# Head norms of the mixer stage: root by exponential of a logarithm, sums by one full matmul

## What is computed

```python
def _norm_f32(x):
    return x * lax.rsqrt(jnp.mean(x * x, axis=-1, keepdims=True) + EPS)
...
h = h + _hybrid_mixer(_rmsnorm(h, mix_norm_w[l]), positions, w_in[l], gdn_conv_w[l], ...,
                      hgrn_norm_w[l], w_out[l])
h = h + _memory_cross_attn(_rmsnorm(h, xattn_norm_w[l]), mem_n, ...)
```

## Time and profile before

| | us |
|---|---|
| median of 3 runs | 2463.57 |
| lowest, highest | 2463.51, 2466.93 |
| the profiled execution, whole | 2461.06 |
| its span of instructions | 2459.3 |
| TensorE busy (matmuls) | 2359.7 (96%) |
| VectorE busy | 1683.5 (68%) |
| ScalarE busy | 681.1 (28%) |
| GpSimd busy | 139.2 (6%) |

### The profile page before, as it was taken

One profiled execution on the slowest core, in us unless ns is written; L12 is line 12 of the kernel. 1 busy time (PEld: TensorE's weight loads), 2 busy tenths in 40 slices (PEclk: granted clock), 3 DMA queues, 4 the chain that ended last, 5 costly groups with the idle time before them and its releaser, 6 DMA issues. The chain is left out here.

```text
span 2459.3 us, 35706 instructions
## 1 busy us (share of the span) xinstructions
PE 2359.7 (96%) x14784; PEld 1911.8 (78%) x14784; DVE 1683.5 (68%) x2643; ACT 681.1 (28%) x1239; POOL 139.2 (6%) x128
## 2 busy tenths in 40 slices
PE   8998859999999999999999899999999999999997
PEld 6886658977888888887755688888888888888886
DVE  6674466756888865558888686666666886666653
ACT  2321363022211101424677503222102113222200
POOL 0000002001000011000211010000010001000001
PEclk9999679999999999999999999999999999999999
DMA  4220003412232364212200171222562541322341
GB/s 180 77 77 3 21 2 129 146 52 78 95 102 94 128 207 145 88 67 82 73 10 2 55 271 65 98 94 95 184 223 89 205 180 61 103 94 95 132 137 65
DMA packets 70193, 252.44 MB, mean 103 GB/s; under 512 B 7792, under 2 KB 8080, under 8 KB 69520
## 3 DMA queue, kind: packets, MB, share of 16 engines
q1 hardware_dynamic: 69744, 249.63, 29.9%
q10 hardware_dynamic: 288, 0.54, 0.1%
HBM read 248.04 MB, written 2.10 MB: 102 GB/s over the span
## 5 line engine op out<-in xcount | busy, mean ns | idle before, releaser
L385 PE MATMUL psum<-rounded_n,rounded_high 128*128 128x512 f32 x1856 | 739.0, 398 | 4.4 <-DVE rounded_n_low L539 1.8
L386 PE MATMUL psum<-rounded_n_low,rounded_high 128*128 128x512 f32 x1856 | 726.3, 391 | 0.0
L387 PE MATMUL psum<-rounded_n,rounded_ring 128*128 128x512 f32 x1856 | 726.2, 391 | 0.0
L339 DVE TENSOR_TENSOR rounded_ring<-ring,rounded_high 128x1024 fp32r<-128x1024 f32 (+1 forms) x360 | 445.7, 1238 | 43.5 <-ACT rounded_high L322 31.5
L385 PEld LDWEIGHTS psum<-rounded_n,rounded_high 128*128 128x128 f32 x1856 | 350.6, 189 | 85.2 <-issue 7.2
L386 PEld LDWEIGHTS psum<-rounded_n_low,rounded_high 128*128 128x128 f32 x1856 | 350.7, 189 | 76.5 <-issue 5.5
L387 PEld LDWEIGHTS psum<-rounded_n,rounded_ring 128*128 128x128 f32 x1856 | 350.4, 189 | 73.7
L337 DVE CAST rounded_high<-ring 128x1024 fp32r<-128x1024 f32 (+1 forms) x347 | 248.8, 717 | 187.3 <-PE psum L387 180.1
L385 PE MATMUL psum<-rounded_arena,rounded_high 128*128 128x512 f32 x720 | 281.3, 391 | 4.4 <-DVE rounded_ring L339 4.4
L387 PE MATMUL psum<-rounded_arena,rounded_ring 128*128 128x512 f32 x720 | 281.0, 390 | 0.0
L386 PE MATMUL psum<-rounded_arena,rounded_high 128*128 128x512 f32 x720 | 280.9, 390 | 0.0
(11 more groups left out here) (494 smaller groups left out, 2752.4 us busy)
## 6 DMA issues: line engine op xcount, KB each, us to landing
ring<-in_w_up SPq DMA_DIRECT2D x132, 512.0 KB, 3.3
ring<-in_w_down SPq DMA_DIRECT2D x48, 512.0 KB, 3.6
n_low<-in_mod_w SPq DMA_DIRECT2D x48, 512.0 KB, 5.4
arena<-in_mod_w SPq DMA_DIRECT2D x48, 512.0 KB, 5.1
ring<-in_w_ab_in SPq DMA_DIRECT2D x37, 512.0 KB, 3.3
ring<-in_w_mix_in SPq DMA_DIRECT2D x31, 512.0 KB, 3.4
ring<-in_w_sc_in SPq DMA_DIRECT2D x24, 512.0 KB, 4.8
ring<-in_w_down SPq DMA_DIRECT2D x24, 384.0 KB, 3.2
```

The costliest lines, as they stand in the source:

```text
L339: nc.vector.tensor_tensor(self.rounded(raw), raw, self.rounded(high), ALU.subtract).then_inc(self.weights_split, 1)
L385: self.nc.tensor.matmul(out, w_high, x_high, start=first, stop=False)
L386: self.nc.tensor.matmul(out, w_high, x_low, start=False, stop=False)
L387: return self.nc.tensor.matmul(out, w_low, x_high, start=False, stop=last)
```

## The change

The sums of a tile come from one matmul: `head_ones` (a 128x128 matrix with ones in the two 64x64 blocks of the diagonal) as weights, all 512 columns of the squares moving. So each head's sum stands on all of its 64 partitions at once, in a whole PSUM bank, and the eight spreading matmuls of a tile go, with `last_norms`. ScalarE then works on whole tiles: `norm_root(n)` takes the Ln of each tile's bank (with eps and 1/64 inside) into its square room, and afterwards the Exp with scale -0.5 in place, which is the inverse root. VectorE's reciprocal goes, and `norm_value` reads the square room where it read a PSUM bank. Each sum has a bank of its own among six; the sums of norms 2 and 3 stand behind `use(15)` and wait until the delta rule's banks are copied out (`delta_kept`); those of 4 and 5 wait for the Ln of norms 0 and 1 (`logged`), and `square(4)`, `square(5)` for the values of norms 0 and 1 (`valued`), as they reuse rooms.

```diff
--- before.py
+++ after.py
@@ -1469,9 +1469,8 @@
     ends, factors, crossable = (k.sem("cr_" + s) for s in ("ends", "factors", "ready"))
     ks, r_ready, solved, u_ready, done_out, grown, s_ready, delta_kept = (
         k.sem("ds_" + s) for s in ("ks", "r", "solved", "u", "out", "grown", "s", "kept"))
-    squared, summed, rooted, scaled, spread, valued, rounded, finished = (
-        k.sem("hn_" + s) for s in ("squared", "summed", "rooted", "scaled", "spread", "valued", "rounded",
-                                   "finished"))
+    squared, summed, logged, rooted, valued, rounded, finished = (
+        k.sem("hn_" + s) for s in ("squared", "summed", "logged", "rooted", "valued", "rounded", "finished"))
     steps, asteps = k.sem("mx_steps"), k.sem("mx_asteps")
 
     past = k.previous
@@ -1523,39 +1522,18 @@
     r, u_ = k.sum_sq[:, 0:256], k.sum_sq[:, 256:512]
     groups = ((0, 4), (4, 6), (6, 8))
     square_rooms = k.square_rooms + k.square_rooms
-    SUM_BANK = (D0,) * 6 + (G0 + 2,) * 2
-    SPREAD_BANK = (D0 + 1, D0 + 2, D0 + 3, D0 + 1, D0 + 2, D0 + 3, G0 + 3, G0)
+    SUM_BANK = (D0, D0 + 1, D0 + 2, D0 + 3, D0, D0 + 1, G0 + 2, G0 + 3)
 
     def norm_sums(pe, i):
         pe.wait_ge(squared, i + 1)
         if i == 0:
             pe.wait_ge(u_ready, TT)
-        pair = k.const("head_ones")[:, HD - 1:P]
-        for c in range(TT):
-            at = 8 * i + 2 * c
-            last = nc.tensor.matmul(k.psum[:, SUM_BANK[i], at:at + HD + 1],
-                                    square_rooms[i][:, c * P:(c + 1) * P], pair, start=True, stop=True)
-        last.then_inc(summed, 1)
-
-    def norm_spread(pe, i):
-        n = 1 if i < 4 else i // 2
-        pe.wait_ge(scaled, n)
-        if i == 0:
+        if i == 2:
             pe.wait_ge(delta_kept, 2)
-        if i >= 3:
-            pe.wait_ge(valued, i - 2)
-        for c in range(TT):
-            for s in range(2):
-                col = 8 * i + 2 * c + s
-                last = nc.tensor.matmul(k.psum[head_rows(s), SPREAD_BANK[i], c * P:(c + 1) * P],
-                                        k.rstd[:, col:col + 1].broadcast_to([P, HD]), k.const("ident"),
-                                        start=True, stop=True)
-        last.then_inc(spread, 1)
-
-    def last_norms(pe, kk):
-        if kk == 1:
-            for i in (6, 7):
-                norm_spread(pe, i)
+        if 4 <= i < 6:
+            pe.wait_ge(logged, i - 3)
+        nc.tensor.matmul(k.psum[:, SUM_BANK[i], :], k.const("head_ones"), square_rooms[i], start=True, stop=True
+                         ).then_inc(summed, 1)
 
     def sync(sp):
         first = k.first_tile["mix_out"]
@@ -1894,26 +1872,19 @@
         scan_out(3)
         use(13)
         use(14)
-        for i in range(4):
+        for i in range(2):
             norm_sums(pe, i)
         use(15)
-        use(16)
-        for i in range(3):
-            norm_spread(pe, i)
-        use(17)
-        use(18)
-        norm_spread(pe, 3)
-        use(19)
+        for i in (2, 3):
+            norm_sums(pe, i)
+        for x in range(16, 20):
+            use(x)
         use(20)
         for i in (4, 5):
             norm_sums(pe, i)
-        use(21)
-        use(22)
-        for i in (4, 5):
-            norm_spread(pe, i)
-        for x in range(23, len(uses)):
+        for x in range(21, len(uses)):
             use(x)
-        pe.wait_ge(valued, 4)
+        pe.wait_ge(logged, 6)
         for _ in range(8):
             nc.tensor.matmul(k.psum[:, D0 + 1, 3 * P:T], k.const("ident"), k.const("ones"), start=True, stop=True)
         for i in (6, 7):
@@ -2038,14 +2009,18 @@
 
         def square(i):
             if i >= 4:
-                act.wait_ge(summed, i - 3)
+                act.wait_ge(valued, i - 3)
             nc.scalar.activation(square_rooms[i], k.o[:, MIX_ORDER[i], :], ACT.Square).then_inc(squared, 1)
 
         def norm_root(n):
             a, b = groups[n]
-            act.wait_ge(summed, b)
-            nc.scalar.activation(k.rstd[:, 8 * a:8 * b], k.psum[:, SUM_BANK[a], 8 * a:8 * b], ACT.Sqrt,
-                                 bias=k.const("eps"), scale=1.0 / HD).then_inc(rooted, 1)
+            for i in range(a, b):
+                act.wait_ge(summed, i + 1)
+                nc.scalar.activation(square_rooms[i], k.psum[:, SUM_BANK[i], :], ACT.Ln, bias=k.const("eps"),
+                                     scale=1.0 / HD).then_inc(logged, 1)
+            for i in range(a, b):
+                act.wait_ge(logged, i + 1)
+                nc.scalar.activation(square_rooms[i], square_rooms[i], ACT.Exp, scale=-0.5).then_inc(rooted, 1)
 
         def high_part(i):
             act.wait_ge(valued, i + 1)
@@ -2301,15 +2276,10 @@
             low = k.mix_low[j]
             link(nc.vector.scalar_tensor_tensor(low, k.o[:, j, :], k.mix_gain[j], low, ALU.mult, ALU.mult))
 
-        def norm_scale(n):
-            a, b = groups[n]
-            dve.wait_ge(rooted, n + 1)
-            nc.vector.reciprocal(k.rstd[:, 8 * a:8 * b], k.rstd[:, 8 * a:8 * b]).then_inc(scaled, 1)
-
         def norm_value(i):
             low = k.mix_low[MIX_ORDER[i]]
-            dve.wait_ge(spread, i + 1)
-            nc.vector.tensor_tensor(low, low, k.psum[:, SPREAD_BANK[i], :], ALU.mult).then_inc(valued, 1)
+            dve.wait_ge(rooted, i + 1)
+            nc.vector.tensor_tensor(low, low, square_rooms[i], ALU.mult).then_inc(valued, 1)
 
         def low_part(i):
             j = MIX_ORDER[i]
@@ -2369,7 +2339,6 @@
         use(14)
         gate(3)
         use(15)
-        norm_scale(0)
         use(16)
         k.split_until(dve, k.first_tile["mix_out"] + 1)
         use(17)
@@ -2388,7 +2357,6 @@
         use(21)
         low_part(2)
         low_part(3)
-        norm_scale(1)
         use(22)
         k.split_until(dve, k.first_tile["mix_out"] + 2)
         use(23)
@@ -2403,13 +2371,12 @@
         dve.wait_ge(taken, TURNS + len(uses))
         for i in (6, 7):
             gate(i)
-        norm_scale(2)
         for i in (6, 7):
             norm_value(i)
         for i in (6, 7):
             low_part(i)
 
-    return Stage(sync, tensor, scalar, vector, pool, finished=finished, last_norms=last_norms)
+    return Stage(sync, tensor, scalar, vector, pool, finished=finished)
 
 
 def residual_product(k, name, rhs, gain=None, mod=None, before=None, next_gain=None,
@@ -2430,8 +2397,7 @@
 
     def tensor(pe):
         if mixed is not None:
-            k.product(pe, name, rhs, T, out, inputs_ready=mixed.signals["finished"], lead=2,
-                      beside=lambda kk: mixed.signals["last_norms"](pe, kk))
+            k.product(pe, name, rhs, T, out, inputs_ready=mixed.signals["finished"], lead=2)
         elif attended is not None:
             k.product(pe, name, rhs, T, out, inputs_ready=attended.signals["done"], lead=2,
                       banks_free=(attended.signals["moved"], PRODUCT_BANKS))
```

## The result

| | before | changed |
|---|---|---|
| median of 20 runs each, same chip | 2462.83 | 2466.88 |
| lowest, highest | 2460.1, 2466.97 | 2463.77, 2470.33 |
| ratio, with 95% interval | | 1.0015 (1.0009 to 1.0021) |
| the profiled execution | 2461.06 | 2465.36 (span 2463.6) |

The change costs 3.7 us by the ratio (2.2 to 5.2). That is within the 0.2% that I called no change, and the interval excludes zero all the same: it is a small loss. The forecast was +1.5 on the profiled execution; there it is +4.3. Between the two medians it is +4.05, since that of the kernel before is 2462.83 over 20 runs and was 2463.57 over the three that I started from.

The account below looks back on a forecast made before the run. A ring of VectorE, ScalarE and TensorE was taken to set the pace at the changed stage. Terms 0 + 2.2 - 2.1 + 1.4 = +1.5 us gave 2462.6 profiled, 2465.1 median; range 2460.5 to 2468.8.

Parts of the forecast that it names:

- Prices: ScalarE's assumed costs: 1.28 us per table load, 0.59 per Ln out of PSUM, 0.52 per Exp.
- The rule I weighed: Skill page's table switch: 1.28 us load plus 1.38 drain, 2.66 in all; it would make the sum +2.9.
- First group: 323 to 338 us: ScalarE's longer chain delays VectorE 3.4 us, just covered since TensorE's spreads go; counted 0.
- Second group: 347 to 352 us: loads, Ln and Exp ahead of the decay are fully exposed, as VectorE already waits; +2.2 us.
- Third group: 375 to 383 us, output product's start: removed spreads shorten TensorE's queue and ScalarE's longer work stays covered; -2.1 us.
- Memory's root: 427 to 433 us: a table load now stands ahead of the root and is fully exposed; +1.4 us.
- Rival (b): TensorE's clock rises only behind the values ScalarE waits for, which take twice as long; +6.2, 2469.8 us; 4%.
- Rival (a): ScalarE's longer chain isn't covered in the first group and costs the whole 3.4 us; +4.9, 2468.5 us; 9%.
- Rival (c): One function set holds both Ln and Exp, so no group needs a load; -3.7, 2459.9 us; 4%.
- Rival (d): TensorE's time counts as such, being 96% busy, so all 11.4 us of spreads are won; 2452 us; 3%.

Follow-up runs that it names:

- e2: Changed kernel with a one-column Sqrt on ScalarE behind the fourth mix_out tile, so the memory root's table loads early; 2463.93 us, ratio 1.0003.
- e4: Changed kernel with 14 empty matmuls put where the first group's spreads stood, ahead of the first cross parts; 2470.89 us, ratio 1.0023.
- e3: Changed kernel with the second group's root and its values moved behind the last cross part, where ScalarE idles; 2460.56 us, ratio 0.9986.
- e7: Kernel before (Sqrt, reciprocal, spreads) with its second group's root moved behind the last cross parts; 2460.2 us, ratio 0.9986.
- e5: Changed kernel with the memory's transfer issued ahead of the wait for the third unit's values; 2466.83 us, ratio 1.0016.
- e1: Changed kernel with 18 empty matmuls in TensorE's pause behind use(24), to raise its clock for the values; 2466.03 us, ratio 1.0011.
- e6: Changed kernel with four edits: 14 empty matmuls behind use(24), early Sqrt table, second group moved, early memory transfer; 2457.77 us, ratio 0.9975.
- e10: Kernel before with its second group moved and 14 empty matmuls behind use(24); 2453.99 us over 8 runs, ratio 0.9971.

## Why the prediction was right, and where its sum was short

**The code** was right: no change that can be told from 0.2%, and 2466.88 lies in the range. The predicted 2465.1 is 1.8 us too low, and that it is so near is in part luck: the three runs of before that it starts from lay 0.7 us above the median of 20. As a difference the forecast was +1.5 and the measured one is +3.7 to +4.3. My own range, +0.6 to +4.2, holds the first of these and not the second.

**Prices.** The load is 1.28 us everywhere and the next instruction follows after 0.01 to 0.02. Ln out of PSUM and Exp took 2.42 and 2.19 us for four. The rule I weighed, 2.66 us for a switch (the Trainium skill, ScalarE: Activation LUTs, What ACT_TABLE_LOAD costs), doesn't hold here: e2 takes the whole switch away at the memory's root and gets 1.43 us, the load and what little stands beside it.

**First group, 0.** Right, -0.33 between the two profiles, and shown to be the balance that I claimed (e4: +3.24 when TensorE's work is put back). I should have worked out the spreads at either clock: against the three profiles of before it is -0.3 to +1.25, so the zero of the first pair is in part luck.

**Second group, +2.2.** Right: +2.27, 2.2 to 2.3 over all profiles, and gone with the group's move (e3 and e7).

**Third group, -2.1.** Right: -2.20. ScalarE's longer chain stayed under the product. But 0.94 of it is waited away again at the next place, as told below.

**Memory's root, +1.4.** Right: +1.43, and e2 returns it.

**The clock: the step that failed.** Rival (b) had the mechanism and I gave it 4%: "from 363 us on TensorE does in both kernels the same", so the clock would be the same. The profile before had it full at 368 us, and I took that single reading as a property of the kernel. It happens in one of its three profiles that it isn't. I had also written that the clock was at half after the second group's spreads anyway; it was full from 354 us to just short of 360, and only then fell. Its 4.7 us were too much: it is 2.1 between the two profiles, since the clock rises within the values. The cross parts ahead of the values are slower too (2.93 us instead of 2.40; 2.93 also in the third profile of before), which is 0.1 of the second term.

**The wait that I had not looked for.** In the third group I asked only whether the inputs for kk = 6 come in time. What is behind `high_part` and the second table load on ScalarE's queue, the memory's 16 instructions and behind them the cast that VectorE waits for, I had counted at nothing without naming its cover. VectorE already waited there 0.92 us, so there was none, and of a product that came 2.2 us sooner only the 1.26 that the cast gained could be kept. It cost 0.94 in the profile and up to 1.3 in the repeat, and e5 brings 0.7 to 1.05 of it back by the profile.

With both, 1.5 + 2.1 + 0.9 is 4.5 us, and the chain's mean over three profiles of before and two of the changed kernel differs by the same (104.8 and 109.3). The parts of that mean are others, though: the first group +0.4, the values +1.5, the wait +1.1. So the clock's share is known only to about a microsecond. Rival (a) falls: the first group's delay was covered. Rival (c) falls: each group has its two loads. Rival (d) falls: removed spreads pay only where something waited for them, 3.2 us ahead of the first cross parts (e4), which ScalarE used up, and 2.2 in the product, and the time rose.

What stays open: by which of its parts the change lowers the clock, why e1 gives back 2.8 us by the profile and not by the time, and the microsecond of e5. The resolution is bounded, since the rest of the program moves by chance as much (over all these profiles the first group's load starts at 323.2 to 327.6 us, and from the reciprocal to the end it is 2028.4 to 2032.3).

## What to carry to other kernels

Moving work from a busy engine to an idle one is worth what the places say, not what the busy shares say. Here 10.9 us more on an engine that was busy 28% of the time cost 2.3 us in one place, 1.4 in another and nothing by itself in two more, and moving one group to where that engine waits was worth as much in the old way (0.14%) as the choice of its arithmetic (0.15 to 0.17%), and twice that in the new (0.3%). After each lengthened piece, follow the engine's own queue to the next instruction that another engine already waits for. And a function that ends a stage with another table leaves its load in front of the next stage's first root, in code that the diff doesn't show.

## What the hardware showed unexpectedly

In the same kernel the granted clock of one stretch is at either level from one execution to the next. The values took 4.60, 6.41 and 4.61 us in three profiles of the kernel before, and the first spreads 5.12, 3.99 and 3.54. Filling TensorE's idle time with empty matmuls ahead of the stretch (e1, e6, e10) had the clock full in the window from 364 to 366 us in all three profiles, where it was 0.50 to 0.59 in the eleven others, and brought the third unit's copies 0.8 to 1.35 us sooner. The values were then at 4.60 to 4.89 us, but so were they in six of those eleven. In the old way the time fell with it (0.9986 to 0.9971, on two chips, intervals that overlap).
